# RG-LRU gate products of chunks 1 to 3 as three fp32r passes, the convolution's output split by ScalarE and VectorE

## What is computed

```python
xc = causal_depthwise_conv(u_lru, conv_w[l], conv_b[l])      # 4 taps, 512 channels
r = sigmoid(einsum('bshc,hcd->bshd', xh, w_a) + b_a)          # xh: xc in 8 heads of 64
i = sigmoid(einsum('bshc,hcd->bshd', xh, w_i) + b_i)
log_a = -LRU_C * r * softplus(-lam)
a = exp(log_a)
bterm = sqrt(max(-expm1(2.0 * log_a), 0.0)) * (i * xf)
h = scan over positions of  h_t = a_t * h_{t-1} + bterm_t
y_lru = h * gelu(u_gate)
```

## Time and profile before

| what | value |
|---|---|
| median of 3 runs | 912.07 us (911.73 to 912.11) |
| the profiled execution | 911.77 us, its span 910.0 us |
| TensorE, VectorE, ScalarE, GpSimd busy | 98%, 66%, 43%, 30% of the span |
| TensorE's mean granted clock | 0.997 of full |
| gate products (L1740) | 32 records, first at 46.3 us, last at 98.1 us |

### The profile page before, as it was taken

One profiled execution on the slowest core, in us unless ns is written; L12 is line 12 of the kernel. 1 busy time (PEld: TensorE's weight loads), 2 busy tenths in 40 slices (PEclk: granted clock), 3 DMA queues, 4 the chain that ended last, 5 costly groups with the idle time before them and its releaser, 6 DMA issues.

```text
span 910.0 us, 10954 instructions
## 1 busy us (share of the span) xinstructions
PE 893.8 (98%) x3956; PEld 729.8 (80%) x3956; DVE 602.6 (66%) x835; ACT 390.0 (43%) x647; POOL 272.4 (30%) x211
## 2 busy tenths in 40 slices
PE   7999999999999999999999999999999999999996
PEld 5777777888888788888888888888888888888885
DVE  5678895644679855575655656647557975787666
ACT  6679524532565432333323333233325444445455
POOL 1000012534243754555446555464550000000000
PEclk9999999999999999999999999999999999999998
DMA  9010102114010223332233322333229943333324
GB/s 317 8 47 27 43 24 70 48 47 139 0 46 25 81 93 127 93 128 82 93 128 92 128 82 93 128 93 127 81 93 350 406 122 94 103 94 96 100 82 185
DMA packets 93678, 95.91 MB, mean 105 GB/s; under 512 B 5636, under 2 KB 63544, under 8 KB 93624
## 3 DMA queue, kind: packets, MB, share of 16 engines
q1 hardware_dynamic: 83240, 76.32, 24.8%
q10 hardware_dynamic: 10384, 18.88, 7.0%
HBM read 70.81 MB, written 24.38 MB: 105 GB/s over the span
## 4 chain that ended last, share of the span: by engine, by line
PE 95%; DVE 2%; DMA 1%; ACT 1%; POOL 0%; issue 0%; SPq 0%; DVEq 0%; ACTq 0%
PE bank L1835 23%; PE bank L1837 23%; PE bank L1836 23%; PE bank L1721 4%; PE bank L1723 4%; PE bank L1722 4%; PE bank L1665 3%; PE bank L1667 3%; PE bank L1666 3%; PE bank L1740 2%; DMA h<-in_x 1%; PE bank L1751 1%; PE bank L1699 1%; DVE nT_lo L1178 1%; DVE xc L1256 0%; PE bank L1758 0%
## 5 line engine op out<-in xcount | busy, mean ns | idle before, releaser
L653 POOL TENSOR_TENSOR r_lo<-gu_raw,r_hi 128x512 fp32r<-128x512 f32 x84 | 116.8, 1391 | 68.4 <-ACT r_hi L920 68.3
L653 POOL TENSOR_TENSOR r_lo<-wsum_S,r_hi 128x512 fp32r<-128x512 f32 x63 | 98.7, 1567 | 125.2 <-ACT r_hi L920 125.2
L1835 PE MATMUL bank<-T_hi,r_lo 128*128 128x512 f32 x336 | 130.9, 390 | 0.9 <-DVE u L1521 0.9
L1837 PE MATMUL bank<-T_hi,r_hi 128*128 128x512 f32 x336 | 130.7, 389 | 0.0
L1836 PE MATMUL bank<-T_lo,r_hi 128*128 128x512 f32 x336 | 130.7, 389 | 0.0
L1835 PE MATMUL bank<-d_hi,h_lo 128*128 128x512 f32 x308 | 119.8, 389 | 0.0
L1836 PE MATMUL bank<-d_lo,h_hi 128*128 128x512 f32 x308 | 119.8, 389 | 0.0
L1837 PE MATMUL bank<-d_hi,h_hi 128*128 128x512 f32 x308 | 119.8, 389 | 0.0
L920 ACT CAST r_hi<-gu_raw 128x512 fp32r<-128x512 f32 x84 | 52.2, 621 | 131.2 <-PE bank L1837 131.2
L1835 PE MATMUL bank<-nT_hi,r_lo 128*128 128x512 f32 x252 | 98.1, 389 | 0.0
L1836 PE MATMUL bank<-nT_lo,r_hi 128*128 128x512 f32 x252 | 98.0, 389 | 0.0
(11 more groups left out here) (214 smaller groups left out, 1619.3 us busy)
## 6 DMA issues: line engine op xcount, KB each, us to landing
h_raw<-hid_ops ACTq DMA_DIRECT2D x72, 256.0 KB, 2.6
gu_raw<-in_w_ffn_gate SPq DMA_DIRECT2D x22, 512.0 KB, 3.7
gu_raw<-in_w_ffn_up SPq DMA_DIRECT2D x22, 512.0 KB, 4.8
hid_ops<-hid SPq DMA_DIRECT2D x44, 256.0 KB, 2.2
dn<-in_w_ffn_down SPq DMA_DIRECT2D x44, 256.0 KB, 9.8
hid_ops<-hsum_S SPq DMA_DIRECT2D x33, 256.0 KB, 2.5
w_raw<-in_w_in SPq DMA_DIRECT2D x11, 512.0 KB, 3.8
h<-in_x SPq DMA_DIRECT2D x8, 512.0 KB, 6.8
```

The source lines that it names most:

```text
L653: pool.tensor_tensor(lo_of(n)[:], a_block(f, name), f32(hi_of(n)[:]), ALU.subtract)\
L1835: pe.matmul(bank, s_lo, m_hi, start=(opens and j == 0), stop=False, skip_group_check=True)
L1837: ins = pe.matmul(bank, s_hi, m_hi, start=False, stop=(closes and j == n - 1), skip_group_check=True)
```

## The change

The gate products of chunks 1 to 3 are taken in three fp32r passes each; chunk 0 stays in fp32. For that the gate weights of all chunks are split once: ScalarE copies them (`gate_weights_hi`, between evacuate(1, 0) and evacuate(1, 1)), VectorE subtracts (`gate_weights_lo`). The convolution's output of chunk j is split into `xc_hi` by ScalarE (`gates_hi(j)`) and `xc_lo` by VectorE (`gates_lo(j)`); there is one tile of each, so from chunk 2 on both wait for the gate products of the chunk before. gates_hi(1) stands ahead of sigmoids(0, 1), gates_hi(2) and gates_hi(3) between tanh and exp of decay(1) and decay(2). gates_lo(1) and gate_weights_lo() stand behind split_w(3), gates_lo(2) and gates_lo(3) between first_half and recur of the next chunk. The new tiles lie on memory that other tiles have left by then.

```diff
@@ -106,6 +106,12 @@
         y1_hi = at("y1_hi", 152.25, [P, GT, S], F32R)
         y1_lo = at("y1_lo", 168.25, [P, GT, S], F32R)
         sq_scr = at("sq_scr", 196.25, [P, 512])
+        xc_hi = at("xc_hi", 152.25, [P, S], F32R)
+        xc_lo = at("xc_lo", 156.25, [P, S], F32R)
+        gw_hi = [at(f"gw_hi{g}", 180.25 + 2 * g, [P, GT, P], F32R) for g in range(2)]
+        gw_lo = [at(f"gw_lo{g}", 160.25 + 2 * g, [P, GT, P], F32R) for g in range(2)]
         xs2 = [at(f"xs2_{s}", 116 - 4 * s, [P, D]) for s in range(2)]
@@ -235,6 +241,7 @@
         sq_a_ok, sq_half_ok = sem("sq_a_ok"), sem("sq_half_ok")
         fin_act_ok = sem("fin_act_ok")
         psq_ok = sem("psq_ok")
+        gw_hi_ok, gw_lo_ok, xc_hi_ok, xc_lo_ok = (sem(n) for n in ("gw_hi_ok", "gw_lo_ok", "xc_hi_ok", "xc_lo_ok"))
         lsq_ok = sem("lsq_ok")
         ys_hi_ok, wo_hi_ok = sem("ys_hi_ok"), sem("wo_hi_ok")
         raw_ok = sem("raw_ok")
@@ -809,6 +816,8 @@
                 if j > 0:
                     act.wait_ge(scan_ok, j)
                 act.activation(t2, rg[:], ACT.Tanh, scale=sp[:, 6, j:j + 1]).then_inc(t2_ok, 1)
+                if 1 <= j < GT - 1:
+                    gates_hi(j + 1)
                 act.activation(ag[:], rg[:], ACT.Exp, scale=sp[:, 7, j:j + 1]).then_inc(a_ok, 1)
             def root(j):
@@ -827,6 +836,17 @@
                     dst = ssum[0] if p == 0 else rg
                     act.activation(dst[:, half(i)], pg[w % 2][:], ACT.Square, scale=v("pool_scale", p))\
                         .then_inc(psq_ok, 1)
+            def gate_weights_hi():
+                act.wait_ge(small_in, 16 * 5)
+                for g in range(2):
+                    act.copy(gw_hi[g][:], gate_w[g][:]).then_inc(gw_hi_ok, 1)
+            def gates_hi(j):
+                act.wait_ge(xc_ok, j + 1)
+                if j >= 2:
+                    act.wait_ge(gates_ok, 4 * j)
+                act.copy(xc_hi[:], xc[j % 2][:]).then_inc(xc_hi_ok, 1)
             def lru_squares(g):
                 act.wait_ge(lmul_ok, g + 1)
@@ -868,6 +888,7 @@
             evacuate(0, 0)
             evacuate(0, 1)
             evacuate(1, 0)
+            gate_weights_hi()
             evacuate(1, 1)
             split_w(3)
             sigmoids(0, 0)
@@ -876,6 +897,8 @@
                     sigmoids(c - 2, 0)
                 if 0 <= c - 2 < GT:
                     split_w(c + 2)
+                    if c == 2:
+                        gates_hi(1)
                     sigmoids(c - 2, 1)
                     decay(c - 2)
                 evacuate(c, 0)
@@ -1260,6 +1283,18 @@
                         step(ins)
                 ins.then_inc(xc_ok, 1)
+            def gate_weights_lo():
+                dve.wait_ge(proj_ok, after(2))
+                for g in range(2):
+                    dve.wait_ge(gw_hi_ok, g + 1)
+                    dve.tensor_tensor(gw_lo[g][:], gate_w[g][:], f32(gw_hi[g][:]), ALU.subtract).then_inc(gw_lo_ok, 1)
+            def gates_lo(j):
+                dve.wait_ge(xc_hi_ok, j)
+                if j >= 2:
+                    dve.wait_ge(gates_ok, 4 * j)
+                dve.tensor_tensor(xc_lo[:], xc[j % 2][:], f32(xc_hi[:]), ALU.subtract).then_inc(xc_lo_ok, 1)
             def recur(j):
                 dve.wait_ge(t2_ok, j + 1)
@@ -1336,6 +1371,8 @@
             for c in range(NC_IN):
                 if c >= 2:
                     first_half(c)
+                if 2 <= c - 1 < GT:
+                    gates_lo(c - 1)
                 if 0 <= c - 2 < GT:
                     recur(c - 2)
                 if 0 <= c - POOL0 - 2 < GT:
@@ -1346,6 +1383,8 @@
                         softplus()
                     if c == 1:
                         split_w(3)
+                        gates_lo(1)
+                        gate_weights_lo()
                 elif c < GATE0:
                     window_mean(c - POOL0)
                 else:
@@ -1727,8 +1766,11 @@
             def gates(j, i):
-                if i == 0:
-                    pe.wait_ge(xc_ok, j + 1)
+                if i == 0 and j == 0:
+                    pe.wait_ge(xc_ok, 1)
+                elif i == 0:
+                    pe.wait_ge(xc_lo_ok, j)
+                    pe.wait_ge(gw_lo_ok, 2)
                 for g in range(2):
                     n = 4 * j + 2 * i + g
                     if n >= 2:
@@ -1737,8 +1779,12 @@
                         pe.wait_ge(vec_ok, 1)
                         pe.wait_ge(rb_ok, 1)
                         pe.wait_ge(small_in, 16 * 5)
-                    pe.matmul(pg[n % 2][:], gate_w[g][:, j], xc[j % 2][:, half(i)], start=True, stop=True)\
-                        .then_inc(gates_ok, 1)
+                    if j == 0:
+                        ins = pe.matmul(pg[n % 2][:], gate_w[g][:, 0], xc[0][:, half(i)], start=True, stop=True)
+                    else:
+                        ins = three_pass(pg[n % 2][:], [(gw_hi[g][:, j], gw_lo[g][:, j], xc_hi[:, half(i)],
+                                                         xc_lo[:, half(i)])])
+                    ins.then_inc(gates_ok, 1)
             def pool_product(p):
                 pe.wait_ge(d_ok, p + 1)
```

## The result

| kernel | median of its runs | lowest to highest |
|---|---|---|
| before | 911.89 us (10 runs) | 911.02 to 912.30 |
| changed | 914.64 us (10 runs) | 913.21 to 915.71 |

What follows compares the result with a forecast made beforehand. TensorE, busy 98% of the span, was taken to bound the kernel. Stalls of 2.5 and 0.9 less 2.2 saved gave +1.2 us after gates(3, 1), 1.4 by tanh(3): 912.07 + 1.4 = 913.4 us, range 911.8 to 915.2.

Steps and rivals of the forecast that it cites:

- rival D: First stall, before project(3, 0): the pause halves PE's clock, costing 2.2 us on top of 1.4: 915.6; chance 0.12.
- The saving on PE: Six gate groups of chunks 1 to 3: 1.36 us instead of 1.72, 0.37 saved per group, 2.2 us in all.
- The first pause: PE before project(3, 0): stalls 2.5 us because VectorE's inserted subtractions delay first_half(2).
- Chunk 2, hidden: PE at chunk 2's gates: no wait, xc_lo(2) hidden by 0.7 us and the sigmoids of its first half by 0.2.
- Chunk 3, the second stall: PE before gates(3, 0): stalls 0.9 us for xc_lo(3), bounds 0.4 to 1.5, streaming at 91.7.
- What is late next: From tanh(3) to pool_product(1): tanh(3) at 100.9, 1.4 us later, and PE takes over that 1.4 us.
- B: Before gates(3, 0): no second stall, only the first, net +0.3 us: 912.4; chance 0.15.
- C: Before project(3, 0): PE does not stall and the 2.2 us saving comes through: 909.9; chance 0.07.
- E: Gate groups on PE: three passes save nothing, second stall gone, +2.6 us: 914.7; chance 0.04.
- F: Window means on VectorE: more lateness handed on, 0.5 us or more added: 914.1 to 914.6; chance 0.05.

Runs made afterwards that it cites:

- e9a: The changed kernel itself, unedited, profiled in one more execution: 913.65 us.
- e1: The changed kernel with gates_lo(1) and gate_weights_lo() moved behind first_half(2) on VectorE: 911.75 us, ratio 1.0000 to the kernel before.
- e4: The kernel before with only four 128x512 subtractions to unused memory added on VectorE behind split_w(3): 914.24 us.
- e9b: The changed kernel itself, unedited, profiled in a second further execution: 914.09 us.
- e7: As e1, with the copies and subtractions of the convolution's output split by halves of 512 tokens: 910.91 us, ratio 0.9989 to the kernel before.
- e2: As e1, with chunk 3 kept in plain fp32 gate products: 911.28 us, ratio 0.9995 to the kernel before.
- e3: The changed kernel in its own VectorE order, with chunk 3 kept in plain fp32 gate products: 913.09 us, ratio 1.0020 to the kernel before.
- e8: As e7, with chunk 3 kept in plain fp32 gate products: 910.50 us, ratio 0.9985 to the kernel before.

## Why the prediction was right or wrong

The measured median is in the range and its direction is that of the forecast, but the likeliest case was "within 0.2%" at 913.4, and the kernel is 0.3% slower, a result to which I gave 0.31. The point and what was measured meet in part of the executions only: the median of the lower five is 913.42, that of the upper five 915.53, and rival D had 915.6. That the median of all ten is in the range is luck. It is the middle of a gap in which no run lies (913.88 to 915.41), and with one more execution in the upper level it would be above 915.4, outside the range, which ended at 915.2. So the stalls of the forecast are what the traces show, and its clock is wrong for half of the executions; it had named a fall of the clock behind the pause as a sign of being wrong.

**The saving on PE.** Forecast 0.37 us a group, 2.2 for six. In e9a gates(1, 1) and gates(2, 0) are 6.80 us apart where they were 7.21: 0.41, 2.5 for six. Right, a little small: the group saves the 0.36 forecast, and the 24 products behind it save 0.05 (5.44 against 5.49) where I had taken 0.01. The 227 ns a product held. The Trainium skill ("TensorE: Matmul & The Clock Gate", "Wait — 56ns, not 53.3ns?") gives 215.7 ns, which would make a group 1.29 us, and it takes 1.36. The whole saving comes near the 2.6 us that the figure of the Trainium skill gave, but for another reason, the products behind the groups.

**The first pause.** Forecast 2.5 us, measured 2.4 (57.56 against 55.27, with the 0.1 by which e9a starts earlier). Right, and e1 and e4 show both that the order on VectorE makes it and that nothing later gives it back.

**Rival D, the clock.** This is the step that failed. I gave it 0.12 and left the clock out of the sum because of one earlier gap of 2.11 us without a fall, and took the 2.5 us that the clock took to fall at the end of one trace for a fixed length. It is not fixed from one execution to the next: at the end of e9a's trace (PE's last product, then a window) it falls 2.2 us behind the end of that product,

```profile
904.25 0.39 PE L1883 MATMUL bank<-d_hi,h_hi 128*128 128x512 f32 x1
```

```profile
906.00:907.00 1.00, 0.00 (x0) 0.00 (x0) 0.95 (x3) 0.83 (x3) 0.00 (x0) 0.92 0.74 283
907.00:908.00 1.00, 0.00 (x0) 0.00 (x0) 0.64 (x4) 0.20 (x1) 0.00 (x0) 0.50 0.30 119
```

and at the end of e9b's only after 4.8:

```profile
904.68 0.39 PE L1883 MATMUL bank<-d_hi,h_hi 128*128 128x512 f32 x1
```

```profile
908.00:909.00 1.00, 0.00 (x0) 0.00 (x0) 0.90 (x4) 0.48 (x1) 0.00 (x0) 1.00 0.90 348
909.00:910.00 1.00, 0.00 (x0) 0.00 (x0) 0.27 (x1) 0.24 (x1) 0.00 (x0) 0.96 0.46 176
```

With that spread a pause of 2.2 us is met by the fall in some executions and missed by it in others, and the even split of ten runs fits; this is argued from the spread and not shown by an experiment. The price of the fall was forecast at 2.2 us from the length of the low stretch at the end of a trace, where PE has nothing to do. Behind a pause the low stretch was 3.4 us, about eight products at 0.43 instead of 0.227, 1.6 us. The Trainium skill ("TensorE: Matmul & The Clock Gate", "Why this matters for your kernels") warns of idle gaps between bursts of matmuls but puts the danger at longer ones than the 2.2 us at which it came here. The direction of its rule held, and the measurement decides on the length.

**Chunk 2, hidden.** Right for xc_lo(2), for which PE waits nowhere. Wrong for its sigmoids: I had them hidden by 0.2 us, and PE waits 0.35 for them (84.03 in e9a). What I had left out stands on ScalarE, e9a:

```profile
72.43 1.15 ACT L818 ACTIVATE t2b<-rg,sp 128x1024 f32<-128x1024 f32 x1
...
77.64 0.82 ACT L792 ACTIVATE xc<-ub,vec 128x512 f32<-128x512 f32 x1 [0.65 <-DVE ig L1303]
...
89.52 1.05 ACT L849 CAST xc_hi<-xc 128x1024 fp32r<-128x1024 f32 x1 [1.67 <-DVE xc L1279]
...
101.32 1.15 ACT L818 ACTIVATE t2b<-rg,sp 128x1024 f32<-128x1024 f32 x1
```

evacuate(3, 0) (L792, at 77.64) idles 0.65 us for the product ix on VectorE, because it overwrites the tile that ix reads, and ix now stands behind gates_lo(2). I had followed what is queued behind the copy on ScalarE and not who waits for VectorE's instruction behind the subtraction. That delays the sigmoids, the square root and with it convolve(3). In e7, with the copy in halves and only half of the subtraction ahead of ix, evacuate(3, 0) does not wait, and PE's wait shrinks from e1's 0.8 to 0.2 us.

**Chunk 3, the second stall.** Forecast 0.9 us with PE streaming at 91.7; measured 0.75 of idling and the issue at 91.88. Right, some 0.4 late by the same forgotten wait; the second half is issued at 98.82, where I had it streaming at 98.5. e2, e3 and e8 show that this chunk's split is a net loss.

**What is late next.** Forecast tanh(3) at 100.9 and 1.4 us on PE at the end; measured 101.32, and PE's last product 2.0 us later than before (904.25 against 902.36, with the 0.1). pool_product(1) waits 0.2 us for VectorE. The mechanism was right and its size 0.6 short in the traces. 0.5 of that is there at tanh(3) already, and I put it down to the same forgotten wait of 0.65 us. The medians show 1.5 us (913.42 against 911.89), 0.5 less than the traces. So that the lower level lies at the forecast's very figure is partly luck too.

**Rivals B, C and E** are refuted by the stalls in e9a and by the groups of 1.36 us. F was not seen as a cause of its own: most of its extra 0.6 us is there before the window means.

## What to carry to other kernels

Work that is inserted on an engine that works in order is paid by what stands behind it, so list for each inserted instruction the waiters of every instruction behind it, those that wait to overwrite a tile too. Ahead of an instruction with no slack even hidden-looking work costs its full length: here three instructions moved behind a fourth were worth 2.7 us at the median, more than all the passes saved (2.5). Split work that a consumer takes in halves by the same halves, and leave out the chunk whose chain has no room.

## What the hardware showed that I had not expected

A pause of TensorE of 2.2 us halves the granted clock behind it in some executions and not in others of the same kernel: 5 of 10 of the changed kernel, 3 of 8 of e3, 2 of 5 of e4, by their levels of time. The traces taken in both levels (915.71 and e4's 915.95 with 0.50 behind the pause; 913.65, 914.09 and e3's 912.86 with 1.00) carry that. By the traces it cost 1.6 us. The medians of the two levels lie further apart, 2.1 us in the changed kernel, 2.0 in e3 and 1.9 in e4. In the profiles at 915.71 and 913.65 the difference is the start, 0.47 us later in the slow one (46.64 against 46.17). Whether a late start and the fall go together is not shown; e9b starts as late (its pause ends at 58.03) and kept its clock. At 1.0 us the upper level never came in 11 runs, and at 4.0 us the five runs lost some 2.4 us at the median, 2.9 in the one with a trace. So a single run, or a profile taken once, may show either level. Why one execution meets the fall and the next does not is not shown by anything here.
